# The output product by two pairs of units, and GpSimd's additions to h, in a one-core decoder layer

## The reference, cut to what matters

```python
    h = h + merged @ w_out[i]                                   # 256x2048 @ 2048x2048
    v = rms_norm(h, g_mlp[i])
    h = h + jnp.square(jax.nn.relu(v @ w_mlp_up[i])) @ w_mlp_down[i]   # 2048 -> 8192 -> 2048
    h = h + jax.nn.sigmoid(h @ w_ple_gate[i]) * (p[i] @ w_ple_proj[i])
```

## Time and profile before

| | us |
|---|---|
| median of 3 runs | 1551.68 (1551.67 to 1551.78) |
| the profiled execution | 1551.78 |
| its span | 1550.0 |
| PE busy | 1541.4 |
| DVE busy | 1269.4 |
| ACT busy | 955.1 |
| POOL busy | 287.4 |
| output product | 689.6 to 776.55 |
| MLP | 776.55 to 1453.9 |

### The profile page before, as it was taken

How to read it: one execution, slowest core, us unless ns; L and a number is a source line. 1 busy time by engine, 2 the same in 40 slices (tenths; PEclk the granted TensorE clock), 3 DMA queues, 4 the chain that set the end, 5 groups by cost and what they waited for, 6 DMA issues and landing times.

```text
span 1550.0 us, 20497 instructions
## 1 busy us (share of the span) xinstructions
PE 1541.4 (99%) x7105; PEld 1272.5 (82%) x7105; DVE 1269.4 (82%) x1554; ACT 955.1 (62%) x1308; POOL 287.4 (19%) x407
## 2 busy tenths in 40 slices
PE   9999999999999999999999999999999999999998
PEld 8888887878878888888888888888888888888887
DVE  6679988768999867996689888889879888889965
ACT  6564466655444555666778844776458755776754
POOL 0222276543000000000004200330004200423300
PEclk9999999999999999999999999999999999999999
DMA  9765567565666667876656656565655665556663
GB/s 329 265 198 192 156 206 236 191 214 177 195 215 205 190 230 278 277 248 244 200 192 195 197 193 215 190 207 189 202 204 190 204 212 187 189 195 204 229 199 127
DMA packets 93761, 324.17 MB, mean 209 GB/s; under 512 B 10864, under 2 KB 14448, under 8 KB 93296
## 3 DMA queue, kind: packets, MB, share of 16 engines
q1 hardware_dynamic: 93536, 322.88, 62.7%
q10 hardware_dynamic: 144, 0.26, 0.1%
HBM read 312.62 MB, written 10.49 MB: 208 GB/s over the span
## 4 chain that ended last, share of the span: by engine, by line
PE 99%; ACT 0%; ACTq 0%; issue 0%; POOL 0%; DVE 0%; POOLq 0%
PE ps L480 17%; PE ps L481 17%; PE ps L482 17%; PE ps L1033 15%; PE ps L1032 15%; PE ps L1034 15%; PE ps L811 0%; PE ps L1123 0%; PE ps L1122 0%; PE ps L1124 0%; PE ps L814 0%; PE ps L817 0%; PE ps L895 0%; PE ps L920 0%; PE ps L971 0%; PE ps L795 0%
## 5 line engine op out<-in xcount | busy, mean ns | idle before, releaser
L456 ACT ACTIVATE sb<-sb 128x1024 fp32r<-128x1024 f32 x525 | 551.8, 1058 | 465.4 <-PE ps L482 265.4
L463 DVE TENSOR_TENSOR sb<-sb,sb 128x1024 fp32r<-128x1024 f32 x498 | 609.0, 1234 | 171.9 <-ACT sb L456 163.9
L480 PE MATMUL ps<-sb,sb 128*128 128x512 f32 (+1 forms) x1152 | 448.3, 389 | 0.0
L481 PE MATMUL ps<-sb,sb 128*128 128x512 f32 (+1 forms) x1152 | 445.5, 387 | 0.0
L482 PE MATMUL ps<-sb,sb 128*128 128x512 f32 (+1 forms) x1152 | 445.4, 387 | 0.0
L1032 PE MATMUL ps<-sb,sb 128*128 128x512 f32 x997 | 387.8, 389 | 0.0
L1033 PE MATMUL ps<-sb,sb 128*128 128x512 f32 x997 | 387.8, 389 | 0.0
L1034 PE MATMUL ps<-sb,sb 128*128 128x512 f32 x997 | 387.8, 389 | 0.0
L1518 POOL COPY sb<-sb 32x256 f32<-32x256 f32 x160 | 139.7, 873 | 943.0 <-DVE sb L2100 937.0
L480 PEld LDWEIGHTS ps<-sb,sb 128*128 128x128 f32 x1152 | 216.3, 188 | 49.1 <-issue 4.2
L482 PEld LDWEIGHTS ps<-sb,sb 128*128 128x128 f32 x1152 | 216.3, 188 | 44.2
(11 more groups left out here) (274 smaller groups left out, 1066.0 us busy)
## 6 DMA issues: line engine op xcount, KB each, us to landing
sb<-in_w_gate SPq DMA_DIRECT2D x128, 512.0 KB, 3.8
sb<-in_w_up SPq DMA_DIRECT2D x128, 512.0 KB, 3.9
sb<-in_w_down SPq DMA_DIRECT2D x128, 512.0 KB, 4.1
sb<-in_w_mix SPq DMA_DIRECT2D x56, 512.0 KB, 4.1
sb<-in_w_branch SPq DMA_DIRECT2D x32, 512.0 KB, 4.7
sb<-in_w_out SPq DMA_DIRECT2D x32, 512.0 KB, 4.2
sb<-in_w_pg SPq DMA_DIRECT2D x32, 512.0 KB, 4.3
gate_mem<-sb SPq DMA_DIRECT2D x16, 512.0 KB, 5.3
```

Source lines behind the costliest of these rows:

```text
L456: act.activation(whi[:, j % RING, :], raw[:, j % RING, :], ACT.Copy).then_inc(hi_done, 1)
L463: eng.tensor_tensor(wlo[:, j % RING, :], raw[:, j % RING, :], whi[:, j % RING, :].bitcast(F32), ALU.subtract).then_inc(lo_done, 1)
L480: pe.matmul(o, xh, w_h, start=first and k == 0, stop=False)
L481: pe.matmul(o, xh, w_l, start=False, stop=False)
```

## The change

Four things change, all by code that sets the order of instructions.

1. The output product is done as two more pairs, p = -2 and p = -1 of group 0, in the interleaved order of the MLP, with short steps at j = 5 in pair -2 and at j = 2 and 5 in pair -1. They get their own places for sums.
2. h is turned in the way of the other pairs (lane, POOL and ACT copies, `relu[c]`), two quarters in pair -1 and two in pair (0, 0). `unit_hi` and `unit_lo` get a form with `g_mlp` as scale, 4 instructions each. Pair (0, 0) therefore waits at its steps 0, 8 and 12, and its short step is now at j = 2, not 5.
3. In groups 0, 1, 2 DVE writes the sums of the down pairs to `relu[c]`, as in an up pair, and POOL adds them to `h` (`add_unit`). In group 3 and in the output product DVE still adds to `h`.
4. Pair 2 gets its second short step, at j = 2, in groups 0, 1 and 2; in group 3 it keeps the one at j = 5.

```diff
-SHORT = [(2, 5), (2, 5), (5,), (2, 5)]
+SHORT = [(2, 5), (2, 5), (2, 5), (2, 5)]
+SHORT_LAST = (5,)
-SHORT_FIRST = (5,)
+SHORT_FIRST = (2,)
+SHORT_OUT = [(5,), (2, 5)]
+OUTS = len(SHORT_OUT)
 def short_steps(g, p):
-    return SHORT_FIRST if p == 0 and isinstance(g, int) and g == 0 else SHORT[p]
+    if p < 0:
+        return SHORT_OUT[p]
+    if isinstance(g, int) and (g, p) == (0, 0):
+        return SHORT_FIRST
+    return SHORT_LAST if isinstance(g, int) and (g, p) == (NFG - 1, 2) else SHORT[p]
...
 # PE
-            for n in range(NCH):
-                for j in range(TPU):
...
-                    products(pe, U_WO + n, j, g, g % 2, m_hi, m_lo, kj * TK, kj == 0, kj == TPU - 1)
...
-                if first_pair:
-                    pe.wait_ge(tp_lo, TP_H + NCH - 1)
+                if p == -OUTS:
+                    pe.wait_ge(tp_lo, TP_M + NCH - 1)
+                    pe.wait_ge(grp_free, 2 * G_WO - 2)
                 else:
-                    pe.wait_ge(temps_free, g * PAIRS + p)
+                    pe.wait_ge(temps_free, g * PAIRS + (p + OUTS))
...
-                    if first_pair and i == 2 * SHORT_FIRST[0]:
-                        pe.wait_ge(tp_lo, TP_H + NCH)
+                    if first_pair and i in (0, TPU, TPU + TPU // 2):
+                        pe.wait_ge(tp_lo, TP_H + {0: NCH - 2, TPU: NCH - 1}.get(i, NCH))
...
-            for p in range(PAIRS):
+            for p in range(-OUTS, PAIRS):
                 pair_of_units(0, p)
 # ACT
+                if scale is not None:
+                    for k in range(4):
+                        ins = act.activation(dst[:, k, :], relu[c][:, k * S:(k + 1) * S], ACT.Copy, scale=scale[:, k:k + 1])
...
                     if first_pair:
-                        turned(i, TP_H + NCH - 1, side_of(TP_H + NCH - 1))
-                        if i in (2, 4):
+                        if i in (1, 9):
...
-                        if i in (5, 6):
-                            tt = i - 5
+                        if i in (7, 8):
+                            tt = i - 7
...
 # POOL
+            def add_unit(g, n):
+
+                gp.wait_ge(grp_free, g * (4 * NCH) + 2 * (G_FF + NCH + n + 1))
+                hc = h[:, :, n * C:(n + 1) * C]
+                gp.tensor_tensor(hc, hc, relu[n % 2].rearrange("p (t n) -> p t n", t=TT), ALU.add).then_inc(h_added, 1)
+            for q in range(NCH):
+                unit_moves(q)
+            for g in range(NFG):
+                for q in range(NCH):
+                    unit_moves(g * NCH + q + NCH)
+                if g < NFG - 1:
+                    for n in range(NCH):
+                        add_unit(g, n)
 # DVE
+                if scale is not None:
+                    for k in range(4):
+                        ins = v.scalar_tensor_tensor(out=dst[:, k, :], in0=relu[c][:, k * S:(k + 1) * S],
...
                     if first_pair:
-                        if i == 0:
-                            v.wait_ge(grp_free, 2 * (G_WO + NCH))
-                            turn_h(NCH - 1, TP_H)
-                            v.wait_ge(tp_lo, TP_H + NCH - 1)
-                        if i in (1, 3):
-                            up_token_sums(int(i == 1))
+                        if i in (0, 8):
+                            v.wait_ge(tp_lo, TP_H + (3 if i else 2))
+                            kept_token_sums(int(i == 8), v_hi, v_lo, whole, up_raw).then_inc(up_sums, 1)
+                        if i in (2, 10):
...
-                    if i in (13, 14) and not up:
+                    onto_h = not up and (p < 0 or last_group)
+                    if i in (13, 14) and onto_h:
                         c = i - 13
                         linked(v.tensor_tensor(h_part(c), h_part(c), extra[:, c, :, :], ALU.add))
...
-                        if up:
+                        if not onto_h:
+                            if p == PAIRS - 1:
+                                v.wait_ge(h_added, g * NCH + (c + 1))
+                            if p == 0 and not first_pair:
+                                v.wait_ge(h_added, g * NCH + (c + 1 - NCH // 2))
                             ins = v.tensor_tensor(relu[c].rearrange("p (t n) -> p t n", t=TT), m, extra[:, c, :, :], ALU.add)
```

More of the change, by code:

```diff
@@ L124 @@
 SEVEN = (2, 5)
-SHORT = [(2, 5), (2, 5), (5,), (2, 5)]
+SHORT = [(2, 5), (2, 5), (2, 5), (2, 5)]
+SHORT_LAST = (5,)
 SHORT_BEFORE = [sum(len(steps) for steps in SHORT[:p]) for p in range(PAIRS)]
 SHORT_ALL = sum(len(steps) for steps in SHORT)
-SHORT_FIRST = (5,)
+SHORT_FIRST = (2,)
+SHORT_OUT = [(5,), (2, 5)]
+OUTS = len(SHORT_OUT)
+STEPS_OUT = sum(len(steps) for steps in SHORT_OUT)
 def short_steps(g, p):
-    return SHORT_FIRST if p == 0 and isinstance(g, int) and g == 0 else SHORT[p]
+    if p < 0:
[3 more added lines that the diff above has]
+    return SHORT_LAST if isinstance(g, int) and (g, p) == (NFG - 1, 2) else SHORT[p]
 def short_count(g, p, e, times, plus):
-    if isinstance(g, int) and g == 0:
-        return times * (sum(len(short_steps(0, q)) for q in range(p)) + e) + plus
-    return g * (times * SHORT_ALL) + (times * (SHORT_BEFORE[p] + e - len(SHORT[0]) + len(SHORT_FIRST)) + plus)
+    if isinstance(g, int):
+        before = [(h, q) for h in range(g + 1) for q in range((-OUTS if h == 0 else 0), p if h == g else PAIRS)]
+        return times * (sum(len(short_steps(h, q)) for h, q in before) + e) + plus
+    return g * (times * SHORT_ALL) + (times * (STEPS_OUT + SHORT_BEFORE[p] + e - len(SHORT[0]) + len(SHORT_FIRST)) + plus)
 PAIR_ORDER = [(j, c) for j in range(TPU - 2) for c in range(2)] + [(j, c) for c in range(2) for j in (TPU - 2, TPU - 1)]
 UNIT_ENDS = [PAIR_ORDER.index((TPU - 1, c)) for c in range(2)]
-PAIR_STEPS = 45
-LEAD, BETWEEN = TPU - 2, 2
+PAIR_STEPS = 44
 def two_units(lead, between):
@@ L421, in hybrid_layer @@
         half_in = sem("half_in")
+        h_added = sem("h_added")
         pair_step = sem("pair_step")
@@ L1020, in _ @@
                     products(pe, U_BR + n, j, g, g % 2, o_hi, o_lo, j * TK, j % 2 == 0, j % 2 == 1)
[L1022 to L1025, removed]
-                    if m == 0 and kj in (0, TPU - 2):
-                        pe.wait_ge(tp_lo, TP_M + (NCH if kj else NCH - 1))
-                    products(pe, U_WO + n, j, g, g % 2, m_hi, m_lo, kj * TK, kj == 0, kj == TPU - 1)
             def three(o, xh, xl, w_h, w_l, start, stop):
@@ L1095, in pair_of_units @@
                     mm.then_inc(tile_used, 1)
-            for p in range(PAIRS):
+            for p in range(-OUTS, PAIRS):
                 pair_of_units(0, p)
-            with pe.Fori(1, NFG) as g:
+            with pe.Fori(1, NFG - 1) as g:
                 for p in range(PAIRS):
                     pair_of_units(g, p)
-            pe.wait_ge(temps_free, NFG * PAIRS)
+            for p in range(PAIRS):
+                pair_of_units(NFG - 1, p)
+            pe.wait_ge(temps_free, NFG * PAIRS + OUTS)
             for n in range(NCH):
@@ L1519, in _ @@
                 ins.then_inc(half_in, 1)
+            def add_unit(g, n):
[10 more added lines that the diff above has]
+                        add_unit(g, n)
+            for q in range(NCH):
+                unit_moves(NFG * NCH + q + NCH)
             gp.wait_ge(first_var, 1)
```

213 lines of the change are left out of this document (107 added, 106 removed).

## The result

The changed kernel takes **1563.16 us** (median of 4 runs, 1562.97 to 1564.45) against 1551.73 of the kernel before on the same chip (4 runs, 1551.67 to 1551.78): a ratio of 1.0074, 95% interval 1.0061 to 1.0088. Slower, as forecast, and inside the range, but 3.7 us above the predicted 1559.5.

The account below looks back on a forecast made before the run. The prediction took PE's number of matmuls to bound the kernel. Its terms, -4.08 for fewer matmuls, +5.3 for pair 2 and +6.5 for the first pair, summed to +7.7, so 1559.5 us, range 1553.5 to 1564.

Parts of the forecast that it names:

- Both places: Pair 2 of groups 0 to 2 and pair (0, 0), where PE would wait for late inputs; both late was given 67%.
- the rival on POOL: At the start of pairs, POOL's additions to h shut DVE out: 1562 to 1575 us; chance 10%.
- -4.08 us for 18 matmuls: Whole kernel: six more short steps save three matmuls each at 0.2267 us, in full only if PE never waits.
- Pair 2, +5.3: Groups 0 to 2: the second short step makes `unit_lo` late for step 12, 1.77 us per pair; bounds 4.2 to 6.1.
- The first pair, +6.5: Pair (0, 0): late token sums, then late `unit_lo`, delay PE's step 12 by 6.5 us; bounds 5 to 8.5.
- The place of the waits: Pair (0, 0), about 4 us at step 4, 2 before step 12; pair 2, groups 0 to 2, before steps 8 and 12.
- Output pairs at nothing: Pairs -2 and -1 of the output product cost nothing, or under 1 us if their cover is thinner.
- POOL's additions at nothing: Two additions in each of three groups, at a pair's start, taken as 3.1 us each, hide behind 3.0 us to spare.
- All of it hides: Rival for the whole kernel: no new wait of PE anywhere, 1547.7 us; chance 10%.
- only one place costs: Rival: only pair 2 or only the first pair makes PE wait, 1553.0 to 1554.2 us; chance 13%.

Follow-up runs that it names:

- e1: The changed kernel with pair 2 back at one short step (j = 5) in groups 0 to 2: 1559.29 us, ratio 1.0046.
- e8: The kernel before, with the second short step in pair 2 of all four groups: 1557.73 us, ratio 1.0038.
- e3: The changed kernel with 21 unused matmuls filling PE's waits at step 4 of pair (0, 0): 1563.0 us, ratio 1.0073.
- e2: The changed kernel with DVE adding to h in all groups and POOL not at all: 1564.7 us, ratio 1.0080.
- e10: The changed kernel with both `unit_lo` and the second `unit_hi` made earlier in pair 2 of every group: 1560.32 us, ratio 1.0053.
- e9_none: The changed kernel with one short step in pair 2, none in (0, 0), and there later squares and token sums, earlier second `unit_lo`: 1550.51 us, ratio 0.9992.
- e5: The changed kernel with ACT's two squares in pair (0, 0) moved from steps 7 and 8 to 10 and 11: 1560.78 us, ratio 1.0058.
- e4: The changed kernel with the short step of pair (0, 0) at j = 5, its token sums at step 6: 1559.62 us, ratio 1.0052.

## Why the prediction was right, and where its sizes were off

Both places are late, by the mechanisms forecast, and the matmuls are as counted. The terms for both places were too small, though, and each passed its own upper bound: 6.67 against 6.1 for pair 2, 9.03 against 8.5 for the first pair. The upper bounds together give -4.08 + 6.1 + 8.5 = +10.5, 1562.3 us, which is 0.9 under the measured time. The range reached to 1564 for the sake of the rival on POOL, which was false; that the time lies inside it is partly luck. The two terms are 3.9 us short in all, and pair (0, 0) started 0.4 earlier than the count has it; that makes the 3.5 by which the profiled run, 1563.02, is above the forecast.

- **-4.08 us for 18 matmuls: right.** 7087 matmuls, and pairs without a wait are 42.16 us long.
- **Pair 2, +5.3: right in mechanism, 1.4 short.** Waits stand before steps 8 and 12 of (0, 2), (1, 2), (2, 2) and nowhere else, e1 takes them away and e8 makes them alone. The three pairs are 1.87, 2.39 and 2.41 over 42.16, together 6.67. In (1, 2) DVE's end was forecast at 33.05 and came at 33.40. In (0, 2) it came at 32.96, in (2, 2) at 33.42, so DVE explains 0.6 of the 1.4. The rest is that PE loses more than the forecast's difference: from the end of `unit_lo` to the matmul are 0.06 to 0.13 us, and the matmul behind a wait follows after 0.335, not 0.227. That is about 0.2 us in each pair, which the sum left out; only the wait before step 12 adds it, since what the one before step 8 costs is taken up by the second.
- **The first pair, +6.5: the term that failed in size; 9.03.** Its steps one by one. DVE's closing addition was put at 2.4 and started at 3.43. In pair -1 DVE is 1.45 us behind (3, 3) at the last split (44.45 against 42.99 after the pair's start), where I had allowed 0.43 for the second scaled `unit_lo`. The rows below show it: the preparation of the second short step ends 0.57 later than in (3, 3), DVE then waits 0.34 for ACT, which is behind its own scaled form, and the four L2101 take 1.67 for 1.22. That shift goes through: the sums' low half at 17.43 in place of 16.4, PE's next matmul at 17.58, 5.3 us late in place of 4.2. Then PE's clock fell, which no row of before could show. Last, the lists of ACT and DVE ended at 40.78 in place of 38.6. By e3, PE starts step 12 at 40.19 even at full clock; so about 1.6 of the 2.5 us missing are the list, 0.6 the clock, and the rest the start behind a wait and rounding. Of the 1.6, about 1.0 is probably the same shift, and 0.4 is that the two scaled `unit_hi` took 1.7 us each and not 1.5; no run takes these apart.
  DVE in time in pair -1 of the changed kernel (its start is 731.91), then ACT's scaled `unit_hi`, L1342, against 1.04 of the plain form (L1345):

```profile
758.54 2.35 DVE L2136 TENSOR_TENSOR sb<-sb,sb 128x1024 fp32r<-128x1024 f32 x2
...
762.37 1.23 DVE L469 TENSOR_TENSOR sb<-sb,sb 128x1024 fp32r<-128x1024 f32 x1 [0.34 <-ACT sb L462]
763.51 1.67 DVE L2101 SCALAR_TENSOR_TENSOR sb<-sb,sb,sb 128x256 fp32r<-128x256 f32 x4
```

```profile
759.69 1.69 ACT L1342 ACTIVATE sb<-sb,sb 128x256 fp32r<-128x256 f32 x4
```

- **The place of the waits: right, with one left out.** At step 4 they are 2.88 + 2.04, where about 4 was announced, and before step 12 1.07, where about 2 was. That a part would come for the tile's low half (`lo_done`) and not the sums' was not said. Where fewer matmuls were slow (e2, e3, e10) the wait before step 12 is 1.75 to 1.77, and one of 0.53 to 0.60 stands before step 8, which was not forecast; in the changed kernel the slow matmuls hide it.
- **Output pairs at nothing: right.** There is no wait in pairs (0, -2) and (0, -1), and e9_none's median shows the gain that the count gives, though its interval doesn't exclude none.
- **POOL's additions at nothing: right, and the rival false,** though its mechanism is there. They take 2.4 us and 0.9 of waiting for DVE. Together, 3.31, that is above the 2 to 3 announced and only just under the 3.4 from which they would matter by the forecast's working, and DVE is shut out while they run, as the rival said. The idle time at a pair's start takes it up; e2 shows no pair shorter without them.
- **All of it hides, or only one place costs: false.** e1 has the first pair's price alone, e8 pair 2's.

## What to carry to other kernels

Before a few matmuls are saved by elementwise work, replay the list of the engine that has to do it and see when each thing is ready that the bottleneck waits for. That engine's idle time is not all to be had: of the 5.23 us in pair (1, 2) up to step 12, 1.29 stayed idle in the longer list, most of it between operations that depend on each other. When such a replay is taken from a similar stage, go through every instruction at the seam to the stage before: small differences between pair -1 and the stage it was copied from made 1 us, and DVE had too little idle time behind them to take it up. When an operation is moved from DVE to POOL, look at what DVE does meanwhile: here 12 additions worth 14.6 us of DVE's time lengthened its splits, which read two inputs from SBUF, by 12.1.

## What the runs showed of the hardware beyond the forecast

- Waiting of PE brought the clock to its lower level, but not in the same way in kernels that are alike in pair (0, 0). In e1, e2, e5 and e10 the matmuls right behind the wait of 2.9 us were 0.427 us apart; in the changed kernel the six behind it were fast and only those behind the next wait, of 2.04 us, slow. In all 9 were slow in the changed kernel, 16 in e1, 11 in e2, 4 in e5 and 4 in e10. The wait of 1.77 us before step 12 was followed by seven slow matmuls in e2 and by none in e10. None was slow in e4, with 1.84 and 1.80 us of waiting 15 matmuls apart. Why they differ stays open.
- What slow matmuls cost depends on where they stand: in the changed kernel 2.1 us of them cost 0.6, since PE had to wait for ACT and DVE afterwards; those behind the last wait in e2 cost the 1.6 us that they took more (from step 12 on pair (0, 0) lasts 12.64 us there, 11.01 in e10).
- GpSimd's addition of two 128x1024 fp32 inputs takes 2.40 us when no split of DVE is under way at its start and 3.31 when one is. The two-input split that DVE starts next ends 1.08 to 1.09 us after POOL does, in all 12.
